# Differential attention: the eight value units leave the front of the projection and are interleaved, in quarters, with the attention's steps

## The reference, cut to what matters

```python
q, k, v = jnp.split(h @ w_qkv, 3, axis=-1)     # h: 512 x 1024, w_qkv: 1024 x 3072
# rope on the first 16 of every 64 columns of q and k; q scaled by 64 ** -0.5
q, k = ...  # (512, 8 heads, 2 halves, 64)      v: (512, 8 heads, 128)
p = softmax(einsum('bqhcd,bkhcd->bhcqk', q, k))
a = p[:, :, 0] - lam_full * p[:, :, 1]
o = einsum('bhqk,bkhe->bqhe', a, v)
o = rms_norm(o, subln_g) * (1 - lam_init)
return o.reshape(b, s, d) @ w_o
```

## Time and profile before

| | us |
|---|---|
| median of 3 runs | 2882.63 |
| lowest and highest | 2868.81, 2883.25 |
| the profiled execution: its time | 2882.65 |
| its span, first to last instruction | 2881.0 |
| TensorE matmul busy | 2787.8 (97%) |
| VectorE, ScalarE, GpSimd busy | 1428.2, 979.3, 241.9 |
| mean granted TensorE clock | 0.982 of full |
| attention loop, first score to the last step's end | 2332.88 to about 2428 |

### The profile page before, as it was taken

The page is one execution under the profiler, slowest core; times in us unless marked ns, Lnnn a source line. Parts: engine busy times, 40 slices in busy tenths (PEclk is TensorE's granted clock), DMA queues, the critical chain, the costliest instruction groups (busy, mean ns, idle before and its releaser), DMA issues.

```text
span 2881.0 us, 40753 instructions
## 1 busy us (share of the span) xinstructions
PE 2787.8 (97%) x16211; PEld 2251.4 (78%) x16211; DVE 1428.2 (50%) x2059; ACT 979.3 (34%) x1530; POOL 241.9 (8%) x318
## 2 busy tenths in 40 slices
PE   8999888999999999999989999999999989999998
PEld 7855777887887878888878888788887855788887
DVE  4588543666776455554433332433323687433322
ACT  3355443333332232222332222322223256422222
POOL 1000110111000110011110000000001210200000
PEclk8899999999999999999999999999999989999999
DMA  6331001673333645556313323333333310233332
GB/s 233 118 96 59 3 3 42 217 231 114 94 102 92 203 152 189 199 185 202 98 59 98 99 90 97 91 96 95 92 99 94 100 55 1 73 97 99 93 94 70
DMA packets 89844, 311.07 MB, mean 108 GB/s; under 512 B 11632, under 2 KB 12400, under 8 KB 89584
## 3 DMA queue, kind: packets, MB, share of 16 engines
q1 hardware_dynamic: 66928, 232.62, 25.8%
q0 software_dynamic: 22784, 76.56, 8.4%
HBM read 305.99 MB, written 2.10 MB: 107 GB/s over the span
## 4 chain that ended last, share of the span: by engine, by line
PE 89%; DVE 5%; ACT 3%; issue 1%; POOL 1%; DMA 0%; SPq 0%; DVEq 0%; ACTq 0%; POOLq 0%
PE psum L1914 24%; PE psum L1916 24%; PE psum L1915 24%; PE psum L2091 1%; PE psum L2093 1%; PE psum L2092 1%; DVE nmax L1860 1%; PE psum L1989 1%; PE psum L1986 1%; PE psum L1985 1%; PE psum L2293 1%; PE psum L2066 1%; PE psum L2382 1%; PE psum L2263 1%; PE psum L2310 1%
## 5 line engine op out<-in xcount | busy, mean ns | idle before, releaser
L1141 DVE TENSOR_TENSOR w_lo<-stage,w_hi 128x1024 fp32r<-128x1024 f32 (+2 forms) x441 | 518.4, 1176 | 833.4 <-ACT w_hi L654 833.2
L654 ACT ACTIVATE w_hi<-stage 128x1024 fp32r<-128x1024 f32 (+2 forms) x441 | 449.7, 1020 | 1236.8 <-PE psum L1916 1202.6
L1914 PE MATMUL psum<-h_hi,w_hi 128*128 128x512 f32 (+1 forms) x2088 | 817.7, 392 | 3.3 <-DVE w_lo L1141 2.3
L1915 PE MATMUL psum<-h_lo,w_hi 128*128 128x512 f32 (+1 forms) x2088 | 814.9, 390 | 0.0
L1916 PE MATMUL psum<-h_hi,w_lo 128*128 128x512 f32 (+1 forms) x2088 | 814.9, 390 | 0.0
L1914 PEld LDWEIGHTS psum<-h_hi,w_hi 128*128 128x128 f32 (+1 forms) x2088 | 392.9, 188 | 89.1 <-DVE w_lo L1141 4.3
L1916 PEld LDWEIGHTS psum<-h_hi,w_lo 128*128 128x128 f32 (+1 forms) x2088 | 392.8, 188 | 82.8
L1915 PEld LDWEIGHTS psum<-h_lo,w_hi 128*128 128x128 f32 (+1 forms) x2088 | 393.1, 188 | 81.9
L1914 PE MATMUL psum<-hid_hi,w_hi 128*128 128x512 f32 x880 | 343.6, 390 | 6.5 <-DVE hid L1231 6.5
L1916 PE MATMUL psum<-hid_hi,w_lo 128*128 128x512 f32 x880 | 343.1, 390 | 0.0
L1915 PE MATMUL psum<-hid_lo,w_hi 128*128 128x512 f32 x880 | 343.0, 390 | 0.0
(11 more groups left out here) (433 smaller groups left out, 2911.2 us busy)
## 6 DMA issues: line engine op xcount, KB each, us to landing
stage<-in_up SPq DMA_DIRECT2D x220, 512.0 KB, 3.5
mod_w<-in_mod_w POOLq DMA_DIRECT2D x144, 512.0 KB, 4.1
stage<-in_down SPq DMA_DIRECT2D x80, 448.0 KB, 3.3
stage<-in_down SPq DMA_DIRECT2D x40, 512.0 KB, 3.5
stage<-in_w_in SPq DMA_DIRECT2D x24, 512.0 KB, 3.6
stage<-in_w_qkv SPq DMA_DIRECT2D x24, 512.0 KB, 3.6
stage<-in_w_merge SPq DMA_DIRECT2D x16, 512.0 KB, 4.6
turned_n<-in_cmp_w SPq DMA_DIRECT2D x1, 4096.0 KB, 14.2
```

The lines of the kernel that those rows point to most:

```text
L654: act.activation(w_hi[:, c % 2, 0:kt * cols], stage[:, c % NSTAGE, 0:kt * cols], ACT.Copy).then_inc(hi_done, 1)
L1141: dve.tensor_tensor(w_lo[:, c % 2, 0:kt * cols], stage[:, c % NSTAGE, 0:kt * cols], w_hi[:, c % 2, 0:kt * cols].bitcast(F32), ALU.subtract ...
L1914: pe.matmul(dst, wh[:, n], a_hi[:, k], start=start and n == 0, stop=False)
L1915: pe.matmul(dst, wh[:, n], a_lo[:, k], start=False, stop=False)
```

## The change

- The units' order in memory and in the segment becomes k, q, v. The projection loop before the attention now has the 16 key and query units; every index of their rope steps falls by 8.
- Value unit 0 (`v_part(0, 0)` to `v_part(0, 3)`) is multiplied right behind them, into bank 5. Value unit h+1 is multiplied in steps 4h to 4h+3, one part of six matmuls at the end of each step (`v_part`), so that parts stand in steps 0 to 27.
- In step 4h, behind the part, stand the four transposes of value unit h (`turn_v`), now into bank 4, which the steps' own transposes use too; therefore the transposes of step m wait for `vtok_done` as well. The copy into `v_tok` (`take_v`) stands in ScalarE's step 4h behind the exponentials, followed by `hi` of a coming unit.
- VectorE copies unit h out of bank 5 at the head of step 4h (`raw_of_v`), into a new buffer `raw_v`, and has a `lo` in steps 1, 5, ..., 29.
- `sum_o` writes into the head's own bank 6 or 7 instead of bank 5, and `weigh` therefore waits for `ovar_done` instead of `o_done`.
- Two `turn_qk`/`qk_low` less stand in the first steps: `qk_low` of the last but one unit in step 0, `turn_qk` of the last in step 1, its `qk_low` in step 2.

```diff
--- before.py
+++ after.py
@@ -376,9 +376,10 @@
         z_tok, band = phase(("z_tok", [P, TT, D], F32), ("band", [P, 3, 4, P + 16], F32))
-        qk_hi, qk_lo, v_tok, PT, es, ovar = phase(
+        qk_hi, qk_lo, v_tok, PT, es, ovar, raw_v = phase(
             ("qk_hi", [P, 2 * KD, S], F32R), ("qk_lo", [P, 2 * KD, S], F32R), ("v_tok", [P, TT, D], F32),
-            ("PT", [P, 2, TT, S], F32), ("es", [P, DIFF_HEADS * TT, 2], F32), ("ovar", [P, DIFF_HEADS * TT], F32))
+            ("PT", [P, 2, TT, S], F32), ("es", [P, DIFF_HEADS * TT, 2], F32), ("ovar", [P, DIFF_HEADS * TT], F32),
+            ("raw_v", [P, 2, S], F32))
@@ -624,10 +625,10 @@
             pool.wait_ge(swap_zero, 1)
-            for m in range(8, 24):
+            for m in range(2 * KD):
                 pool.wait_ge(raw_done, m + 1)
-                if m >= 10:
-                    pool.wait_ge(roped, 3 * (m - 9))
+                if m >= 2:
+                    pool.wait_ge(roped, 3 * (m - 1))
@@ -1059,18 +1060,19 @@
                 def qk_round(m):
-                    act.wait_ge(roped, 3 * (m - 7))
-                    act.activation(qk_hi[:, m - 8], norm_t[:, m % 2], ACT.Copy).then_inc(qkhi_done, 1)
-
-                for n in range(23):
+                    act.wait_ge(roped, 3 * (m + 1))
+                    act.activation(qk_hi[:, m], norm_t[:, m % 2], ACT.Copy).then_inc(qkhi_done, 1)
+                def take_v(h):
+                    act.wait_ge(post_done, h + 1)
+                    act.activation(v_tok[:, :, h * P:(h + 1) * P],
+                                   psum[:, 4, :].rearrange("p (t n) -> p t n", t=TT), ACT.Copy).then_inc(vtok_done, 1)
+                for n in range(2 * KD):
                     hi(s.first + n + 2)
-                    if 1 <= n <= 8:
-                        act.wait_ge(post_done, n)
-                        act.activation(v_tok[:, :, (n - 1) * P:n * P],
-                                       psum[:, 4 + (n - 1) % 2, :].rearrange("p (t n) -> p t n", t=TT),
-                                       ACT.Copy).then_inc(vtok_done, 1)
-                    if n >= 10:
+                    if n >= 2:
                         qk_round(n - 2)
+                qk_round(2 * KD - 2)
@@ -1106,10 +1108,11 @@
                                            accum_out=es[:, m, c:c + 1]).then_inc(exp_done, 1)
-                    if m == 0:
-                        hi(s.first + 25)
-                    if m < 3:
-                        qk_round(21 + m)
+                    if m == 1:
+                        qk_round(2 * KD - 1)
+                    if m < 4 * DIFF_HEADS and m % 4 == 0:
+                        take_v(m // 4)
+                        hi(s.first + 18 + m // 4)
@@ -1787,35 +1790,39 @@
                 def qk_low(m):
-                    dve.wait_ge(qkhi_done, m - 7)
-                    dve.tensor_tensor(qk_lo[:, m - 8], norm_t[:, m % 2], qk_hi[:, m - 8].bitcast(F32),
+                    dve.wait_ge(qkhi_done, m + 1)
+                    dve.tensor_tensor(qk_lo[:, m], norm_t[:, m % 2], qk_hi[:, m].bitcast(F32),
...
                     dst = norm_t[:, m % 2]
-                    by = 1.0 if m < 16 else HD ** -0.5
-                    if m >= 10:
-                        dve.wait_ge(qklo_done, m - 9)
-                    dve.wait_ge(swapped[m % 2], 64 * ((m - 8) // 2 + 1))
+                    by = 1.0 if m < KD else HD ** -0.5
+                    if m >= 2:
+                        dve.wait_ge(qklo_done, m - 1)
+                    dve.wait_ge(swapped[m % 2], 64 * (m // 2 + 1))
...
                                              op0=ALU.mult, op1=ALU.mult).then_inc(roped, 1)
-                    dve.wait_ge(roped, 3 * (m - 8) + 2)
+                    dve.wait_ge(roped, 3 * m + 2)
...
 
-                for n in range(24):
+                def raw_of_v(h):
+                    dve.wait_ge(unit_done, s.first + 2 * KD + h + 1)
+                    if h >= 2:
+                        dve.wait_ge(post_done, h - 1)
+                    dve.tensor_copy(raw_v[:, h % 2], psum[:, 5, :]).then_inc(raw_done, 1)
+                for n in range(2 * KD):
                     dve.wait_ge(unit_done, s.first + n + 1)
-                    if n >= 10:
-                        dve.wait_ge(roped, 3 * (n - 9))
+                    if n >= 2:
+                        dve.wait_ge(roped, 3 * (n - 1))
                     dve.tensor_copy(raw[:, n % 2], bank(s.tile + n)).then_inc(raw_done, 1)
-                    if n == 23:
-                        continue
                     lo(s.first + n + 2)
-                    if n >= 10:
+                    if n >= 2:
                         qk_low(n - 2)
-                    if n >= 9:
+                    if n >= 1:
@@ -1831,7 +1838,7 @@
                     dve.wait_ge(ossq_done, h + 1)
-                    dve.tensor_tensor(ovar[:, cols], ovar[:, cols], psum[:, 5, cols], ALU.add).then_inc(ovar_done, 1)
+                    dve.tensor_tensor(ovar[:, cols], ovar[:, cols], psum[:, 6 + h % 2, 0:TT], ALU.add).then_inc(ovar_done, 1)
@@ -1853,6 +1860,8 @@
                 for m in range(M + 1):
+                    if m < M and m % 4 == 0:
+                        raw_of_v(m // 4)
@@ -1860,8 +1869,7 @@
                     if m == 0:
-                        lo(s.first + 25)
-                        qk_low(21)
+                        qk_low(2 * KD - 2)
@@ -1873,10 +1881,12 @@
                                                  in1=E[g % 3][:, 0], op0=ALU.mult, op1=ALU.add).then_inc(comb_step, 1)
-                    if 2 <= m <= 3:
-                        qk_low(20 + m)
-                    if 1 <= m <= 2:
-                        turn_qk(21 + m)
+                    if m == 1:
+                        turn_qk(2 * KD - 1)
+                    if m == 2:
+                        qk_low(2 * KD - 1)
+                    if m % 4 == 1:
+                        lo(s.first + 18 + m // 4)
@@ -2544,33 +2554,47 @@
                 s = seg["qkv"]
-                for n in range(24):
+                def v_part(h, part):
+                    c = s.first + 2 * KD + h
+                    if part == 0:
+                        pe.wait_ge(lo_done, c + 1)
+                        if h >= 1:
+                            pe.wait_ge(raw_done, 2 * KD + h)
+                    wh, wl = slot(w_hi, c, KD, P, 2), slot(w_lo, c, KD, P, 2)
+                    for k in range(2 * part, 2 * part + 2):
+                        pe.matmul(psum[:, 5, :], wh[:, k], h_hi[:, k], start=k == 0, stop=False)
+                        pe.matmul(psum[:, 5, :], wh[:, k], h_lo[:, k], start=False, stop=False)
+                        last = pe.matmul(psum[:, 5, :], wl[:, k], h_hi[:, k], start=False, stop=k == KD - 1)
+                    if part == 3:
+                        last.then_inc(unit_done, 1)
+                def turn_v(h, turned_p):
+                    pe.wait_ge(raw_done, 2 * KD + h + 1)
+                    if turned_p:
+                        pe.wait_ge(pt_done, turned_p)
+                    for tt in range(TT):
+                        last = pe.transpose(psum[:, 4, tt * P:(tt + 1) * P], raw_v[:, h % 2, tt * P:(tt + 1) * P], ident)
+                    last.then_inc(post_done, 1)
+                for n in range(2 * KD):
...
                         product(s.first + n, 0, range(KD), (h_hi, h_lo), s.tile + n, True, True)
-                    if 1 <= n <= 8:
-                        m = n - 1
-                        pe.wait_ge(raw_done, m + 1)
-                        if m >= 2:
-                            pe.wait_ge(vtok_done, m - 1)
-                        for tt in range(TT):
-                            last = pe.transpose(psum[:, 4 + m % 2, tt * P:(tt + 1) * P],
-                                                raw[:, m % 2, tt * P:(tt + 1) * P], ident)
-                        last.then_inc(post_done, 1)
-
-                pe.wait_ge(vtok_done, 8)
+                for part in range(4):
+                    v_part(0, part)
...
                     if m == 0:
-                        pe.wait_ge(raw_done, 23)
-                    if m == 1:
-                        pe.wait_ge(raw_done, 24)
+                        pe.wait_ge(raw_done, 2 * KD)
@@ -2582,8 +2606,9 @@
                         pe.wait_ge(pt_done, 4 * h + 4)
+                        pe.wait_ge(vtok_done, h + 1)
                         if h >= 2:
-                            pe.wait_ge(o_done, h - 1)
+                            pe.wait_ge(ovar_done, h - 1)
@@ -2591,10 +2616,8 @@
                     pe.wait_ge(osq_done, h + 1)
-                    if h >= 1:
-                        pe.wait_ge(ovar_done, h)
                     for tt in range(TT):
-                        last = pe.matmul(psum[:, 5, TT * h + tt:TT * h + tt + 1], o_sq[h][:, tt * P:(tt + 1) * P],
+                        last = pe.matmul(psum[:, 6 + h % 2, tt:tt + 1], o_sq[h][:, tt * P:(tt + 1) * P],
@@ -2637,6 +2660,7 @@
                             pe.wait_ge(pt_done, g)
```

(7 more changed lines are left out.)

## The result

The changed kernel takes 2854.38 us (median of 5 runs, 2853.6 to 2869.64), the kernel before 2872.78 us (5 runs, 2868.81 to 2883.25): ratio 0.9948, 95% interval 0.9926 to 0.997. That is 14.9 us faster by the ratio (8.6 to 21). A second set gives 2855.83 us (10 runs) and ratio 0.996 (0.9942 to 0.9978). Forecast were 9.1 us less and 2873.6 us, with a range down to 2860. The forecast gain lies in the first interval, though two fifths short of its centre; the time lies outside the range.

The account below looks back on a forecast made before the run. TensorE, busy 97% of the span, was taken as the bound, with a VectorE-made hole in the first attention steps. -42.0 + 29.8 - 0.3 + 0.5 + 1.4 + 1.5 = -9.1 us, so 2873.6; 8-in-10 range 2860 to 2883.

Parts of the forecast that it names:

- The front: Projection before the attention: seven value units and eight sets of transposes leave TensorE's path, -42.0 us.
- Steps 0 to 6: First attention steps: TensorE's work 19.4 us plus 3.7 idle behind VectorE's rope queue, 23.1 against 23.45, -0.3 us.
- Steps 7 to 27: Rest of the loop: 21 steps with parts of 1.46 us, `sum_o` and value transposes, 86.2 against 56.4, +29.8 us.
- 1.4 for the bank: Later heads: `turn_v` shares a bank with the steps' transposes, 0.2 us of wait in each of seven heads, +1.4.
- 1.5 for the clock: Step 4: TensorE's idle time makes the granted clock fall once for about 3 us, +1.5 us.
- the 1.4 that the forecast had set as a sign of being wrong: Loop: parts start to start over 1.7 us or under 1.4 would show the forecast wrong.
- step 28's transposes: Behind the parts: the transposes of `turn_v` in step 28 cost +0.5 us.
- The starting point: Whole kernel: the gain of 9.1 us was taken from the profiled execution, 2882.65 us, giving 2873.6.
- Rival 1: Loop's start: VectorE isn't late, no idle time or slow clock; gain 15.75 to 18.6 us, 2867 to 2864; chance 0.24.
- Rivals 2 and 3: 2: each change-over costs 0.25 us more, chance 0.11; 3: bank 4's wait costs 1.2 per head, chance 0.10; both 2880.6.
- Rival 4: Loop: the clock stays low; 17 us low leaves a gain of 2, half the loop low gives 2898; chance 0.07.
- Rival 5: Loop: TensorE's gaps take the parts in, 41 us more gain, about 2833; chance 0.02.

Follow-up runs that it names:

- experiment 3: Changed kernel with value units 0 and 1 both multiplied in front of the loop; ratio 0.9952 to the kernel before, stage 214.46 us.
- experiment 8: Changed kernel without 161 of the 168 matmuls of value units 1 to 7, copies and transposes kept; 2836.16 us, one run.
- experiment 9: Changed kernel with 48 unused matmuls added in the compression stretches, three in each round; median 2868.04 us, ratio 0.9974 to the kernel before.

## Why the prediction was right and wrong

**The front, -42.0:** measured -42.0.

**Steps 0 to 6, -0.3:** measured -0.2, and for the reason given. Score 4 and the first part of unit 2 wait 1.2 and 1.7 us, 3.0 before rounding against the 3.4 forecast, and experiment 3 shows the rope queue behind it. That it comes out to a tenth is luck: the waits were forecast too long, and the parts too short where a score comes next, without a `weigh` in the step. This one, in step 1, takes 1.58 us to the next score, not 1.46:

```profile
2295.51 0.50 PE L2566 MATMUL psum<-h_hi,w_hi 128*128 128x512 f32 x1
...
2297.09 0.50 PE L2601 MATMUL psum<-qk_hi 64*128 64x512 f32 x2
```

**Steps 7 to 27, +29.8, with 1.4 for the bank and 1.5 for the clock: 32.7.** Measured +27.9, 4.8 less. The part, taken at 1.46 from the row behind the loop, takes 1.39: 1.5 us less over 21 parts. That is also under the 1.4 that the forecast had set as a sign of being wrong, if only just. The bank's wait is not there at all in these steps: 1.4 us less. It came in step 29, behind them, 0.5 us, where no part covers it (experiment 8: 8.1 us without the parts). The clock didn't fall in step 4 of the two profiled executions of the changed kernel: 1.5 us less. It can fall, though: it did in that of experiment 9, and there it cost what the forecast had put down for it (1.4 us). The last 0.4 are mostly the five sets of value transposes, 0.43 us each and not 0.49.

**The rest.** Steps 28 to 30 are 0.6 us longer (0.5 forecast for step 28's transposes; the wait of step 29 comes on top, and a wait of 0.3 us for the squares in before's step 29 is gone). Behind score 31, 0.6 us are gained that I hadn't counted. Half of this is the wait of the last `sum_o` for the variance of the head before, which the change took out together with the move out of bank 5. Before it had this line, and after there is no such wait:

```profile
2435.81 1.02 PE L2597 MATMUL psum<-cst,c_act 128*128 128x1 f32 x8 [0.30 <-DVE ovar L1834]
```

All this leads from 9.1 to the 14.2 us of the stage.

**The starting point** is the step that put the time outside the range: "Against the profiled execution (2882.65, which is the median's 2882.63) that is 2873.6 us". The kernel before has two groups of times 14 us apart; the three runs at hand were two of the upper and one of the lower, and the median of three fell into the upper. The changed kernel's median fell into the lower one. Subtracting 9.1 from the lower group's 2867.5 would have given 2858.4, which is 3.5 above what the changed kernel's lower group shows, and the range around it would have held the measured time. The 14.4 us between the three runs were read as what a measurement can't tell; they were two values, and the low clock at 60 to 95 us stood in the trace, in a window that I didn't open since the change doesn't touch it.

**The rivals.** Rival 1 (VectorE isn't late) gave the size, 15.8, by luck, with a wrong mechanism: VectorE was late. Rivals 2 and 3 fall with the part at 1.39 and the bank's wait at 0.5 in all. Rival 4, a clock that stays low in the new loop, didn't occur: 1.00 from 2207 to 2399 in the first profile and through the loop in the second, and the fall in experiment 9 lasted 3.4 us. A longer low clock does occur where the parts are lumped (0.84 over the first seven steps). Rival 5, hidden parts: the steps are 1.39 us longer with a part, so next to nothing is hidden in an undisturbed step; but steps 7 to 27 pay only 18 us for 29 us of parts, as they stand where TensorE would otherwise wait for the value units' own copies.

The Trainium skill (TensorE: Matmul & The Clock Gate, "HAM oscillation — how this bites in real kernels") ties the fall of the clock to idle time of TensorE. For the attention's first steps before (TensorE busy 13.8 of 24 us, granted clock 0.64), and for the lumps (0.84 after waits of 2.1 and 3.8 us), the rows agree. For the compression stretch they don't: TensorE was busy 5.00 of each 5 us when the clock fell, with matmuls of few columns. There the measurement decides.

## What to carry to other kernels

Work that needs one engine alone, cut into parts of a step's slack and set at the end of each step, fills both the hole at a loop's start and the waits of the loop itself; the same work in one lump lost 12.4 us here, nearly all of the stage's gain, half of it in the first steps. Cost an insertion from start to start of its neighbours, and count what came along with it (copies, roundings) on the other engines, since the inserted work may be what covers it. Before a forecast of a time, and not only of a difference, look at the spread of the runs at hand: if it is two values, find the stretch of the trace that makes them, however far from the change it is.

## What the runs showed of the hardware

The granted clock can fall to its low level while TensorE is never idle: in a loop of eight matmuls of 32 columns and three of 512. Both profiled executions of the upper group show it, and 3 of 15 runs of the changed kernel and 9 of 32 of the one before lie in that group. In the first profile of the changed kernel it stayed low to the end of that loop and 5 us on, 27 us in all, at a cost of 12.9 us. Just before the fall stood eight matmuls with only two columns (59.8 to 60.7 us), but they stand there in the executions without a fall too. One more matmul of 512 columns to a round left 2 of 20 runs in the upper group, three more left none of 12. What decides between executions of the same program stays open.
